# Latent pages spread over more of the pair loop and into the first gate tiles, with the gate stage's input and weights in buffers of their own

## The reference

```python
xn = _rmsnorm(x, norm_pre)
(qa, kvc, kvs, kvw, gn, ga, qd, kvd, krp, gb, ma, mb) = jnp.split(xn @ w_in, IN_OFFSETS, axis=-1)
# sparse branch: compressed, selected and window attention, mixed by sigmoid(gn)    -> o_a
# latent branch, for the 8 new tokens over the paged latent cache c_all, kr_all:
s = (jnp.einsum('bqhc,bsc->bhqs', q_lat, c) + jnp.einsum('bqhr,bsr->bhqs', q_pe, kr)) * MLA_SCALE
o_lat = jnp.einsum('bhqs,bsc->bqhc', softmax(s), c)
o_b = jnp.einsum('bqhc,chv->bqhv', o_lat, w_kv_up[..., MLA_NOPE:])
pa = (o_a * jax.nn.silu(ga)) @ w_proj_a
pb = (o_b * jax.nn.silu(gb)) @ w_proj_b
h = jax.nn.sigmoid(ma) * pa + jax.nn.sigmoid(mb) * pb
y = x + _rmsnorm(h @ w_out, norm_post)
```

## Time and profile before

| what | value |
|---|---|
| median of 3 runs | 918.73 us |
| profiled execution | 913.32 us |
| its span, first to last instruction | 911.2 us |
| TensorE matmul busy | 783.6 us (86%) |
| VectorE busy | 317.6 us (35%) |
| ScalarE busy | 181.4 us (20%) |
| granted TensorE clock, mean | 0.923 |
| moved by DMA | 170.31 MB, mean 187 GB/s |

### The profile page before, as it was taken

The page is one execution under the profiler, slowest core; times in us unless marked ns, Lnnn a source line. Parts: engine busy times, 40 slices in busy tenths (PEclk is TensorE's granted clock), DMA queues, the critical chain, the costliest instruction groups (busy, mean ns, idle before and its releaser), DMA issues.

```text
span 911.2 us, 15016 instructions
## 1 busy us (share of the span) xinstructions
PE 783.6 (86%) x5839; PEld 525.0 (58%) x5839; DVE 317.6 (35%) x1023; ACT 181.4 (20%) x519; POOL 111.9 (12%) x125
## 2 busy tenths in 40 slices
PE   6999998578968889757767677799999999999994
PEld 2444443463545556534545445488888888888442
DVE  2100001579444666444335253842010110102244
ACT  0400000431304554222223132311010000000111
POOL 0221121020022302231322221000000000000000
PEclk9999999879987999898888797889799999999998
DMA  8898557660053647999998898802022004202001
GB/s 325 332 405 349 205 206 296 220 261 3 1 186 123 201 152 252 327 320 322 313 332 284 311 319 308 352 1 93 1 93 78 15 1 185 93 1 103 37 24 48
DMA packets 59848, 170.31 MB, mean 187 GB/s; under 512 B 7465, under 2 KB 11714, under 8 KB 52994
## 3 DMA queue, kind: packets, MB, share of 16 engines
q1 hardware_dynamic: 50178, 120.97, 36.8%
q0 software_dynamic: 9600, 48.38, 14.2%
HBM read 164.99 MB, written 8.52 MB: 190 GB/s over the span
## 4 chain that ended last, share of the span: by engine, by line
PE 68%; DMA 10%; DVE 8%; SPq 6%; issue 5%; ACT 2%; DVEq 0%; ACTq 0%
PE bank L1125 19%; PE bank L654 12%; PE bank L1130 6%; PE bank L1138 6%; DMA ring<-latent 5%; SPq L475 5%; DMA XG<-latent 4%; PE bank L668 3%; PE bank L994 3%; PE bank L979 3%; PE bank L878 2%; PE bank L796 1%; PE bank L946 1%; PE bank L956 1%; ACT projP L1157 1%
## 5 line engine op out<-in xcount | busy, mean ns | idle before, releaser
L1125 PE MATMUL bank<-XG,ring 128*128 128x260 f32 x768 | 173.5, 388 | 0.0
L1125 PEld LDWEIGHTS bank<-XG,ring 128*128 128x128 f32 x768 | 147.6, 193 | 23.4 <-issue 0.3
L654 PE MATMUL bank<-W,XG 128*128 128x494 f32 x256 | 110.9, 592 | 3.6 <-DMA W<-w_attn 3.6
L654 PEld LDWEIGHTS bank<-W,XG 128*128 128x128 f32 x256 | 49.1, 194 | 63.0 <-issue 61.9
L528 POOL DMA_INDIRECT KRR<-krT,idxi x64 | 60.4, 944 | 188.4 <-PE bank L983 173.5
L1262 ACT ACTIVATE projP<-bank,W 128x128 f32<-128x128 f32 (+3 forms) x96 | 49.9, 524 | 117.5 <-DVE W L1740 117.2
L1740 DVE CUSTOM_DVE_ANT_0 bank<-bank,maskb 128x128 f32<-128x128 f32 (+3 forms) x96 | 46.1, 511 | 72.4 <-PE bank L878 71.8
L1977 DVE SCALAR_TENSOR_TENSOR W<-W,bank 128x260 f32<-128x260 f32 x32 | 13.6, 425 | 146.4 <-PE bank L1130 146.4
L979 PE MATMUL bank<-ring,projP 128*32 128x128 f32 x768 | 31.6, 315 | 38.1 <-DMA ring<-latent 37.9
L878 PE MATMUL bank<-W 64*128 64x128 f32 (+7 forms) x192 | 52.7, 525 | 1.4 <-ACT projP L1262 1.4
L979 PEld LDWEIGHTS bank<-ring,projP 128*32 128x32 f32 x768 | 24.3, 125 | 42.8 <-issue 42.4
(11 more groups left out here) (348 smaller groups left out, 1004.4 us busy)
## 6 DMA issues: line engine op xcount, KB each, us to landing
ring<-latent SPq DMA_DIRECT2D x192, 256.0 KB, 4.7
XG<-latent SPq DMA_DIRECT2D x64, 256.0 KB, 4.6
ring<-w_gate SPq DMA_DIRECT2D x12, 1024.0 KB, 9.2
W<-w_attn SPq DMA_DIRECT2D x16, 494.0 KB, 9.4
ring<-win SPq DMA_DIRECT2D x8, 512.0 KB
o_win<-win SPq DMA_DIRECT2D x1, 4088.0 KB
XG<-xT SPq DMA_DIRECT2D x4, 520.0 KB, 8.2
XG<-xT SPq DMA_DIRECT2D x1, 2080.0 KB, 7.9
```

What stands on the lines that cost most here:

```text
L654: mm = pe.matmul(bank[2 * (u % 2) + n][:, 0:GW], XG[:, k * TOK + tl * P:k * TOK + (tl + 1) * P], W[:, w:w + GW], start=(k == 0), stop=(k = ...
L1125: mm = pe.matmul(bk[:, 0:HALF], job(n)[:, at + k * 256:at + k * 256 + P], XG[:, k * TOK + hf * HALF:k * TOK + (hf + 1) * HALF], start=(k = ...
```

## The change

- **Latent units.** 26 of the 32 start in the pair loop, in two of every three steps from step 11 on (11, 12, 14, 15, 17, 18, ... 47, 48). The other six, and the two that only make outputs, stand ahead of the tiles `v = 0` to `7` of the tail. Their maximum, exponential, transpose, copy and fold go with them, and so does the merge that follows the last one.
- **Gate input.** It goes to `X2`, in the part of `W` that held `qmT`. SP loads it after job 8, when pair 15 has been used; VectorE scales one `k` in each of the steps 27 to 34.
- **Gate weights.** They come in 12 loads of 1 MB into two buffers `gate_w[0]` and `gate_w[1]`, where `kmT` was. Load `g` waits until both tiles of load `g - 2` are done. SP issues loads 0 and 1 after job 23, load 2 ahead of jobs 28 and 29, load 3 ahead of jobs 30 and 31.
- **Tail.** The order inside a group becomes mb, mb, ma, ma. The joins `parts`, `coef` (with what was `oad`), `lat` and `obd` (with what was `gate`) follow the tiles 8, 9, 10 and 11. `h`, the tanh and silu buffers and the slots of the projection weights have new places.

```diff
+        X2 = W[:, 4096:4096 + KM * TOK]
+        gate_w = [W[:, 8256 + i * 2048:8256 + (i + 1) * 2048] for i in range(2)]
...
-        TAIL_SLOT = {J_GB: 2, J_GA: 0, J_M0: 1, J_P0: 2, J_M1: 0, J_M2: 1, J_P1: 2, J_M3: 0, J_WO0: 1, J_WO1: 4, J_X: 0}
+        TAIL_SLOT = {J_P0: 2, J_P1: 3, J_WO0: 0, J_WO1: 1, J_X: 2}
...
-        M_AT = 11
+        X2_FIRST = 27
+        N_M, M_FIRST, M_UNITS = 32, 11, 26
+        M_at, SOFT_z, OUT_z, M_z = {}, {}, {}, {}
+        for m in range(M_UNITS):
+            M_at[M_FIRST + m * (PAIRS + 2 - M_FIRST) // M_UNITS] = m
+        for m in range(M_UNITS, N_M + 2):
+            M_z[m - M_UNITS] = m
...
+        tail = [("gb", c) for c in range(4)] + [("ga", c) for c in range(4)]
         for q in range(4):
+            tail += [(kind, c) for kind in ("mb", "ma") for c in (2 * q, 2 * q + 1)]
+            tail += [(kind, c) for c in (2 * q, 2 * q + 1) for kind in ("pb", "pa")]
+        tail += [("wo", x) for x in range(5)]
+        JOIN_AFTER = {8: "parts", 9: "coef", 10: "lat", 11: "obd"}
+        GATE_JOBS = [("gb", 0), ("gb", 1), ("ga", 0), ("ga", 1)] + [(kind, q) for q in range(4) for kind in ("mb", "ma")]
...
 (SP)
+            def gate(g):
+                kind, q = GATE_JOBS[g]
+                if g >= 2:
+                    before_kind, before_q = GATE_JOBS[g - 2]
+                    sp.wait_ge(S["z_ps"], 2 * tile_no[before_kind, 2 * before_q + 1] + 2)
+                sp.dma_start(gate_w[g % 2], t["w_gate"][:, GATE_AT[kind] + q]).then_inc(S[f"gate_w{g % 2}"], 16)
...
+            for m in range(9):
+                latents(m)
             sp.wait_ge(S["o_ps"], 16)
+            sp.dma_start(X2, t["xT"]).then_inc(S["x2_in"], 16)
+            for m in range(9, 24):
+                latents(m)
+            gate(0)
+            gate(1)
+            for m in range(24, 28):
+                latents(m)
             sp.dma_start(w_vT, t["w_v"]).then_inc(S["wv_in"], 16)
+            for g in range(2, 4):
+                gate(g)
+                latents(24 + 2 * g)
+                latents(25 + 2 * g)
+            gate(4)
             proj_half(J_P0, 0)
             proj_half(J_P1, 1)
+            gate(5)
+            w_out(J_WO0, 0)
+            w_out(J_WO1, 1)
+            for g in range(6, 12):
+                gate(g)
...
 (TensorE)
+            for v, (kind, x) in enumerate(tail):
+                if v in M_z:
+                    latents(M_z[v])
                 if v == 0:
                     pe.wait_ge(S["p"], UNITS)
+                    pe.wait_ge(S["xg2"], KM)
...
+                if v in SOFT_z:
+                    dec_transposes(SOFT_z[v])
+                if v in JOIN_AFTER:
+                    join(JOIN_AFTER[v])
...
 (VectorE)
-                if d >= PAIRS - 1:
-                    scale_input(2 * (d - PAIRS + 1))
-                    scale_input(2 * (d - PAIRS + 1) + 1)
+                if 0 <= d - X2_FIRST < KM:
+                    scale_input(d - X2_FIRST)
...
+                if v - 1 in JOIN_AFTER:
+                    join(JOIN_AFTER[v - 1])
+                if v in SOFT_z:
+                    dec_max(SOFT_z[v])
                 for hf in range(2):
+                    if hf == 1 and v in OUT_z:
+                        dec_fold(OUT_z[v])
+                        if OUT_z[v] is chunks[-1]:
+                            merge()
```

More of the change, by code:

```diff
@@ L283, in build @@
         J_TAIL = 56
-        J_GB, J_GA, J_M0, J_P0, J_M1, J_M2, J_P1, J_M3, J_WO0, J_WO1, J_X = range(J_TAIL, J_TAIL + 11)
-        N_JOBS = J_TAIL + 11
-        TAIL_SLOT = {J_GB: 2, J_GA: 0, J_M0: 1, J_P0: 2, J_M1: 0, J_M2: 1, J_P1: 2, J_M3: 0, J_WO0: 1, J_WO1: 4, J_X: 0}
-        slot += [XG[:, 0:JOB], kmT]
+        J_P0, J_P1, J_WO0, J_WO1, J_X = range(J_TAIL, J_TAIL + 5)
+        N_JOBS = J_TAIL + 5
+        TAIL_SLOT = {J_P0: 2, J_P1: 3, J_WO0: 0, J_WO1: 1, J_X: 2}
+        slot.append(XG[:, 0:JOB])
         def slot_of(n):
@@ L357, in build @@
                 c = add("mla", b, i, P, 1, 256, chunks[-1]["n"] if i else None, i == 1, J_MLA + 2 * p2)
-                SOFT_at[M_AT + 2 * p2 + 1], OUT_at[M_AT + 2 * p2 + 3] = c, c
-        N_M = 32
-        MLA_LAST = [c["n"] for c in chunks if c["kind"] == "mla" and c["last"]]
[L363 to L369, removed]
@@ L370, in build @@
-        for q in range(4):
[L371 to L377, removed]
@@ L378, in build @@
-        halves = [(z[0], z[2], hf) for z in ztiles for hf in range(2)]
+                for at, soft, out in ((M_at, SOFT_at, OUT_at), (M_z, SOFT_z, OUT_z)):
+                    for d, m in at.items():
+                        if m == 2 * p2 + 1:
+                            soft[d] = c
+                        if m == 2 * p2 + 3:
+                            out[d] = c
+        MLA_LAST = [c["n"] for c in chunks if c["kind"] == "mla" and c["last"]]
+        tail = [("gb", c) for c in range(4)] + [("ga", c) for c in range(4)]
@@ L380, in evictor @@
+        job_of = {"pa": lambda x: J_P0 + x // 4, "pb": lambda x: J_P0 + x // 4, "wo": lambda x: J_WO0}
+        tile_no = {z: v for v, z in enumerate(ztiles)}
+        last_tile = {J_P0: tile_no["pa", 3], J_P1: tile_no["pa", 7]}
+        halves = [(z[0], z[1], hf) for z in ztiles for hf in range(2)]
         def evictor(kind):
@@ L466, in _, with latents @@
             n_phys = t["latent"].shape[0]
-            for n in range(J_MLA, J_TAIL):
+            def latents(m):
+                n = J_MLA + m
                 slot_free(sp, n)
-                at = 128 + (n - J_MLA) * 8
+                at = 128 + m * 8
                 with ExitStack() as regs:
@@ L996, in latent_outputs, with latents @@
                 mm.then_inc(S["mv_ps"], 1)
+            def latents(m):
+                if m < N_M:
+                    latent_scores(m)
+                if m >= 2:
+                    latent_outputs(m - 2)
             def dec_transposes(c):
@@ L1057, in join @@
                     mm.then_inc(S["mrg_ps"], 1)
-                elif what == "oad":
+                elif what == "coef":
+                    pe.wait_ge(S["coef"], 1)
+                    pe.transpose(bank[5][:, 320:328], mC[0:8, 0:P], C("ident", 0, 8, rows=8)).then_inc(S["coef_ps"], 1)
                     pe.wait_ge(S["pt_by_A"], PAIRS)
@@ L1316, in _ @@
             tanhs = 0
-            for z in tail:
-                if z[0] == "join":
-                    if z[1] == "parts":
-                        act.wait_ge(S["mrg_d"], 1)
-                        act.activation(mE[0:8, :], mD[0:8, :], ACT.Exp).then_inc(S["mrg_e"], 1)
-                    continue
-                kind, n, x = z
-                v = tile_no[kind, x]
-                m = P if x < TILES else DEC
+            for v, (kind, x) in enumerate(tail):
+                m = P if x < TILES else DEC
+                if v - 1 in SOFT_z:
+                    dt_copy(SOFT_z[v - 1])
+                if v in SOFT_z:
+                    dec_exp(SOFT_z[v])
+                if JOIN_AFTER.get(v - 1) == "parts":
+                    act.wait_ge(S["mrg_d"], 1)
+                    act.activation(mE[0:8, :], mD[0:8, :], ACT.Exp).then_inc(S["mrg_e"], 1)
                 for hf in range(2):
@@ L1933, in join @@
                     ins.then_inc(S["olat"], 1)
-                elif what == "gate":
+                elif what == "obd":
                     def decode(o):
```

121 lines of the change are left out of this document (46 added, 75 removed).

## The result

| | before | after |
|---|---|---|
| median, us (8 runs each) | 919.57 (915.08 to 930.51) | 927.59 (925.32 to 933.53) |
| profiled execution, its span, us | 913.32, 911.2 | 933.53, 931.7 |
| granted TensorE clock, mean | 0.923 | 0.905 |
| first exponential of step 10, the last step without a latent unit, us | 345.9 | 361.8 |
| from there to the first gate tile (the loop), us | 249.0 | 213.1 |

The ratio is 1.007, with a 95% interval of 1.0041 to 1.0099. The change makes the kernel slower by 0.7%, where a gain of 1.7% was forecast. The profiled executions show where the time went. The loop did get shorter, by 36 us; forecast were 60. The tail got longer by 40.5; forecast were 44. And 16 us were lost ahead of the first latent unit, in code that the change does not touch.

The account below looks back on a forecast made before the run. DMA engines were taken to bound the pair loop and TensorE the tail. The tail starting 59.9 us earlier, less 43.8 taken back (16.2 work, 21.6 waits, 6 clock), gave -16.1 from 918.7: 903 us, range 888 to 916.

Parts of the forecast that it names:

- 12.4 us of work fits beside them: Pair loop: engine work of three steps with two units fits beside two page jobs 14.2 us apart; period taken 6.9.
- the 3.19 us taken for a step without a unit: Pair loop: engine time of a step holding no scores of a unit, from four such steps taking 12.75 us.
- the 10.1 predicted for the input and two gate loads: Pair loop: loads now ahead of page jobs delay them, 5.1 us for the input and 5.0 for two gate loads.
- the 6.6 to 7.1: Pair loop: range in us for the period of a unit, outside which the prediction called itself wrong.
- The waits in the tail: Tail, tiles 2 and 4: TensorE waits for page jobs held behind gate loads in SP's order, two of 10.8 us.
- the lower bound: Tail: least length of each page-job wait, 5.1 us for the first MB plus 2 x 2.5 for the job, 10.1.
- The clock in the tail: Tail: work behind each of the two waits runs at 1.2 GHz, 3 us each, 6 in all.
- The work moved into the tail: Tail: moved units' TensorE work counts whole, 15.2 us, plus 0.6 for `outputs(30)` and 0.4 for `obd`: 16.2.
- the start of the tail: End of the loop: the tail starts at 535.0 us instead of 594.9, 59.9 us earlier.
- The base: Whole kernel: the profiled execution, 913.3 us, lay 5.4 under the median; the forecast was taken against the median, 918.7.
- The clock takes the loop: Rival, pair loop: more work at 1.2 GHz makes the kernel over 1% slower, needing a period of 8.1 us; chance 0.10.
- Within 1%: Rival, whole kernel: gain lost in small pieces (period 7.10, open scaling, clock), -5.4 us, 913; chance 0.20.

Follow-up runs that it names:

- `a_sem`: The changed kernel with two old input-load semaphores in place of its two new ones; 895.15 us, 0.985 of the kernel before.
- `a_order`: The changed kernel with SP issuing jobs 28 to 31 ahead of the gate loads that wait for a tile; 873.55 us, 0.963 of the kernel before.
- `a_order_again`: Repeat of the changed kernel with jobs 28 to 31 issued ahead of the waiting gate loads; 871.60 us, 0.960 of the kernel before.
- `a_kr1`: The changed kernel with one key gather of the four per chunk, used four times; run twice: 900.22 and 900.77 us, 0.973 and 0.977 of the kernel before.
- `b0_third`: The kernel before, unchanged, run for its trace; one execution, 920.89 us, with 61 of 202 updates late.
- `a_shift`: The changed kernel with units in the first and third of each three steps; 921.63 us, 1.000 of the kernel before.
- `a0_fourth`: The changed kernel run again, unchanged; 927.75 us, 1.007 of the kernel before.
- series 1: The measurement series of the main result, changed kernel against the kernel before: 927.59 against 919.57 us, ratio 1.007.
- series 3, 5 and 6: Follow-up series of the changed kernel and its variants, with late updates in its profiles; the kernel before took 925.53, 920.91 and 921.88 us.
- `a0`: The changed kernel run again, unchanged; 928.15 us, 1.004 of the kernel before.
- series 3 and 4: Two follow-up series of variants against the kernel before, which took 925.53 us in the first and 909.27 in the second.
- `b0`: The kernel before run again, untouched, for a second trace; 908.64 us, ratio 0.999, no late update.

## Why the prediction was wrong

**The loop.** The step that failed is "12.4 us of work fits beside them", with its bounds of 6.2 to 7.10 us a unit: it held the 3.19 us taken for a step without a unit, and in after such a step took 4.70 us on average. ScalarE's first exponentials of two following steps with no unit between them, in after, then in `a_sem`:

```profile
455.01 0.47 ACT L1288 ACTIVATE projP<-bank,W 128x256 f32<-128x256 f32 x1 [1.35 <-issue]
...
460.27 0.58 ACT L1288 ACTIVATE projP<-bank,W 128x384 f32<-128x384 f32 x1 [1.43 <-DVE W L1766]
```

```profile
417.27 0.37 ACT L1288 ACTIVATE projP<-bank,W 128x128 f32<-128x128 f32 x1 [1.89 <-DVE W L1766]
...
419.85 0.37 ACT L1288 ACTIVATE projP<-bank,W 128x128 f32<-128x128 f32 x1
```

Such a step took 5.3 us here in after and 2.6 in `a_sem`. Summed over the twelve between the exponentials of steps 12 and 46 it is 56.4 and 38.5 us: 17.9 of the 19.8 us by which the loops differ. The 22 steps with a unit took 126.3 and 126.2 us. It is the same in the other profiles of the changed kernel without the shift: the twelve took 53.6 to 57.4 us in the six with late updates, and 38.1 to 38.7 in `a_sem`, `a_order` and `a_order_again`, which had none, and in the two of `a_kr1`. My reading is that such a step has no work of a unit behind which a late update could hide: its small products go to and fro between three engines, and late updates are waited for. At the end of the loop one lies open on the chain of waits of after:

```profile
564.90 4.57 another core or an unknown queue
...
569.67 0.60 ACT projP L1183
...
570.41 1.59 PE bank L921 x16
```

Why the kernel before does not pay is told by its waits for pages. In the loop of `b0_third`, with late updates:

```profile
PE bank L980 <- DMA ring<-latent: 37.1, 18, 3.7
PE bank L980 <- DMA XG<-latent: 9.1, 5, 3.2
```

```profile
ACT projP L1158 <- remote: 35.8, 14, 3.8
```

Its engines wait about as long for late updates as after's, but it still has 46.2 us of waits for pages, 12.4 fewer than the trace of before (58.6), and a delay ahead of a page that has not landed costs nothing. The change brings these waits down to 22.9 us in `a_sem`; in after 3.2 are left (the two lines `PE bank L1001` above). This reading fits the loops without the shift, but `a_shift` shows that it isn't the whole: there the steps without a unit were short again (3.0 us on average, 2.4 from step 26 to step 27), and a step with a unit took 6.0 us in place of the 5.6 of `a0_fourth`.

Where no update is late, the term itself was right: the twelve steps without a unit took 3.21 us each in `a_sem`. From the exponential of step 13 to that of step 46, 22 units, it took 162.0 us; less the 10.1 predicted for the input and two gate loads that is 6.90 a unit, as predicted. No run shows the 10.1 us by themselves, so only the sum is confirmed. After took 177.4, or 7.60 by the same count, outside the 6.6 to 7.1 that the prediction named as its sign of being wrong. The tail, counted from the scores of unit 26, starts at 537.3 in `a_sem` and not at 535.0: unit 4 was read at 372.6 instead of 372.0, unit 25 came 158.4 us behind it instead of 156.5, and what follows unit 25 took 6.3 us, where 6.5 were said.

**The waits in the tail.** Predicted were two of 10.8 us; measured 10.9 and 11.0 in after, with the chain as foretold. The Trainium skill ("DMA: Bandwidth & Descriptors", section Bandwidth) has a figure of 6.15 us for 1 MB issued from GpSimd; by it, an estimate, each would have been 1.1 us longer than the lower bound. By the trace here the gate loads, issued from SP, landed in less:

```profile
W<-w_gate SPq DMA_DIRECT2D x12, 1024.0 KB, 4.8
```

**The clock in the tail.** Predicted were 6 us. TensorE is busy 320.1 us in `a_sem`'s tail, 322.0 in after's and 317.0 in `a_order_again`'s, which has the same work and no wait for a page: 3.1 and 5.0.

**The work moved into the tail.** Predicted were 16.2 us. `a_order_again`'s 317.0 is 12.6 over the 304.4 of the earlier trace rows; with the 1.9 of the scores and outputs that stand ahead of the first tile, 14.5.

**The sum.** In `a_sem` it comes out as said: a span of 894.0 us where 895.1 followed from the terms, and 0.985 of the kernel before where the forecast was 903 of 918.7, 0.983. That the span comes so near is in part luck: the clock in the tail and the moved work were put 2.9 and 1.7 us too high, the start of the tail 2.3 us too early. In after two things are added: 15.9 us ahead of the units, which the kernel before pays too in such a series, and 19.8 in the loop, which it doesn't. The other 2.0 us are in the tail.

**The base.** I noted that the profiled execution lay 5.4 us under the median and went on. It had no late update, and the executions timed beside it most likely did: the kernel before took 919.57 us over all of series 1, much as in series 3, 5 and 6. Trace and median were then of two conditions.

**The rivals.** "The clock takes the loop" was the slower one. The clock did fall in the loop, to 0.86 against 0.92 in `a_sem`, and TensorE's busy time rose by 11.4 us, to 166.3. But it came with the late updates: of the profiles of series 3, `a0` has 0.89 and 160.3 us, and `a_kr1`, with one gather in place of four, 0.92 and 154.9. How much of the 19.8 us went by way of the clock is not shown. The period of 8.1 us that the rival needed, counted as the 7.60 above, was not reached. "Within 1%" had a chance of 0.20 and covers the ratio of 1.007, but by other steps: period 7.10 and 5.4 us faster. None of the rivals named what happened.

**What stays open.** Why a series has late updates and another not. It isn't the chip: series 3 and 4 ran on the same one. All four series with the changed kernel as it stands had them, and the two without it did not. As `b0_third` had them too, that could only work from one kernel on another, and no run here tells it from chance. Nor is it shown by what path a gather delays an update, or why not every gather does: in after none of TensorE's 24 updates from 30 to 170 us is late, beside the gathers there.

## What to carry to other kernels

Spreading work over more steps removes waits for transfers, and with them slack that hid small delays between engines; count what those waits cover before spending them. In a queue that runs in order, put a load that waits for a buffer behind those that don't: here that alone was worth 22 to 24 us. And where the profiled execution lies away from the median, find out what differs before adding anything to either.

## What the runs showed that I had not expected

While GpSimd issues indirect gathers, TensorE's semaphore updates can come up to 4.2 us after the modelled end of the work in the loop of after, and once 5.0 us ahead of it; those of ScalarE and VectorE were never over 0.5 us late there. Short matmuls are slowed themselves. In the kernel before, the chain of waits of `b0` has 1.01 us for 32 small ones:

```profile
271.69 1.01 PE bank L920 x32
```

In `b0_third`, with the gathers of line 529 beside them, they were spread from 275.28 to 280.58. The update of line 912, for which VectorE waited, came 4.8 us late:

```profile
275.77 0.94 POOL L529 DMA_INDIRECT XG<-slc,idxi  x1 [0.30 <-issue]
...
276.53 0.45 PE L920 MATMUL bank<-projD,cst 8*32 8x64 f32 x6 [0.28 <-issue]
...
277.01 0.94 POOL L529 DMA_INDIRECT XG<-slc,idxi  x1 [0.30 <-issue]
277.26 0.45 PE L920 MATMUL bank<-projD,cst 8*32 8x64 f32 x6 [0.28 <-issue]
...
280.19 0.22 DVE L1779 TENSOR_TENSOR bank<-bank,cst 128x48 f32<-128x48 f32 x1 [5.99 <-remote]
```

In `b0` the same gathers ran at the same place, from 271.05 us on, and the 32 were done from 271.62 to 272.70.
